# Products of two constant tiles ahead of waits in a two-layer hybrid decoder trunk

## The reference

```python
def _rmsnorm(x, w):
    return x * rsqrt(mean(x * x, axis=-1) + 1e-6) * w

def _layer(x, state, p):
    f = _swiglu(_rmsnorm(x, p['ffn1_norm_pre']), w_gate, w_up, w_down)     # 1024 -> 2816 -> 1024
    x = x + 0.5 * _rmsnorm(f, p['ffn1_norm_post'])
    m, new_state = _token_mixer(_rmsnorm(x, p['mix_norm_pre']), *state, p)
    x = x + _rmsnorm(m, p['mix_norm_post'])
    f = _swiglu(_rmsnorm(x, p['ffn2_norm_pre']), ...)
    x = x + 0.5 * _rmsnorm(f, p['ffn2_norm_post'])

def _token_mixer(h, ...):
    proj = h @ w_in
    # three recurrent branches over chunks of tokens, each with a state:
    # gated delta rule (4 heads), gated linear attention (4 heads), SSD (8 heads);
    # each output is normalised and gated
    merged = g0 * (o_gdn @ w_br_gdn) + g1 * (o_gla @ w_br_gla) + g2 * (o_ssd @ w_br_ssd)
    return merged @ w_out, new_state
```

## Time and profile before

| | |
|---|---|
| median of three runs | 3268.22 us |
| profiled execution | 3272.43 us |
| its span | 3270.6 us |
| mean granted clock of TensorE | 0.98 |
| PE busy | 3132.8 us, 96% |
| PEld busy | 3039.1 us, 93% |
| POOL busy | 1586.6 us, 49% |
| DVE busy | 1409.6 us, 43% |
| ACT busy | 769.3 us, 24% |

### The profile page before, as it was taken

The page is one execution under the profiler, slowest core; times in us unless marked ns, Lnnn a source line. Parts: engine busy times, 40 slices in busy tenths (PEclk is TensorE's granted clock), DMA queues, the critical chain, the costliest instruction groups (busy, mean ns, idle before and its releaser), DMA issues. The chain is left out here.

```text
span 3270.6 us, 66003 instructions
## 1 busy us (share of the span) xinstructions
PE 3132.8 (96%) x26830; PEld 3039.1 (93%) x26830; DVE 1409.6 (43%) x2212; ACT 769.3 (24%) x1515; POOL 1586.6 (49%) x948
## 2 busy tenths in 40 slices
PE   7999999999989999999999999999999899999998
PEld 7999999987779999999999999999877899999998
DVE  5332086647752225331153311955587522343312
ACT  2111033324441122111031110332344311221110
POOL 6655555600036554655555655655000356555553
PEclk9999999999979999999999999999999899999999
DMA  4222222200142221222222222222002323222222
GB/s 146 89 88 85 85 83 83 84 7 2 58 144 88 89 97 66 89 88 84 73 95 90 83 88 75 94 78 78 7 2 74 138 89 97 79 78 90 82 89 64
DMA packets 80595, 261.15 MB, mean 80 GB/s; under 512 B 8720, under 2 KB 12688, under 8 KB 79760
## 3 DMA queue, kind: packets, MB, share of 16 engines
q1 hardware_dynamic: 80112, 257.82, 23.9%
q10 hardware_dynamic: 288, 0.49, 0.1%
HBM read 243.70 MB, written 14.58 MB: 79 GB/s over the span
## 5 line engine op out<-in xcount | busy, mean ns | idle before, releaser
L620 POOL TENSOR_SCALAR wh<-raw 128x1024 fp32r<-128x1024 f32 (+2 forms) x236 | 243.5, 1032 | 1121.8 <-DMA raw<-in_merge 547.3
L622 POOL TENSOR_TENSOR wl<-raw,wh 128x1024 fp32r<-128x1024 f32 (+2 forms) x236 | 554.1, 2348 | 30.9 <-POOL wh L620 1.4
L622 POOL TENSOR_TENSOR wlx<-raw,whx 128x1024 fp32r<-128x1024 f32 (+2 forms) x236 | 546.7, 2316 | 30.9 <-POOL whx L620 0.2
L660 PE MATMUL ps<-hh,wh 128*128 128x272 f32 x2300 | 480.9, 290 | 27.8 <-POOL wl L622 12.8
L660 PE MATMUL ps<-hh,whx 128*128 128x272 f32 x2356 | 490.6, 290 | 0.0
L664 PE MATMUL ps<-hh,wlx 128*128 128x272 f32 x2356 | 487.2, 288 | 0.0
L662 PE MATMUL ps<-hl,whx 128*128 128x272 f32 x2356 | 487.0, 288 | 0.0
L664 PE MATMUL ps<-hh,wl 128*128 128x272 f32 x2300 | 477.3, 289 | 0.0
L662 PE MATMUL ps<-hl,wh 128*128 128x272 f32 x2300 | 477.0, 289 | 0.0
L620 POOL TENSOR_SCALAR whx<-raw 128x1024 fp32r<-128x1024 f32 (+2 forms) x236 | 243.5, 1032 | 469.6 <-PE ps L664 469.6
L660 PEld LDWEIGHTS ps<-hh,wh 128*128 128x128 f32 x2300 | 363.8, 190 | 30.5 <-issue 16.8
(11 more groups left out here) (450 smaller groups left out, 5276.5 us busy)
## 6 DMA issues: line engine op xcount, KB each, us to landing
raw<-in_up SPq DMA_DIRECT2D x176, 512.0 KB, 3.2
raw<-in_win SPq DMA_DIRECT2D x76, 512.0 KB, 3.2
raw<-in_merge SPq DMA_DIRECT2D x96, 384.0 KB, 3.0
raw<-in_down SPq DMA_DIRECT2D x64, 512.0 KB, 3.5
raw<-in_down SPq DMA_DIRECT2D x32, 384.0 KB, 3.1
raw<-in_wout SPq DMA_DIRECT2D x16, 512.0 KB, 3.2
states<-in_in_gdn SPq DMA_DIRECT2D x2, 2048.0 KB, 7.8
proj<-in_in_ssd SPq DMA_DIRECT2D x2, 2048.0 KB, 8.6
```

Source lines behind the costliest of these rows:

```text
L620: pool.tensor_scalar(hi, src, 1.0, 1.0, MULT, MULT).then_inc(hi_done, 1)
L622: pool.tensor_tensor(lo, src, hi.bitcast(F32), SUB).then_inc(lo_done, 1)
L660: pe.matmul(out, high, mh_[:, c], start=a, stop=False)
```

## The change

A helper `keep_busy(bank, count, c)` is added to PE's program. It multiplies `ones` (128x128) by the identity (128x128) in float32 `count` times, each into the same 128 columns of a bank of PSUM whose contents the next real product overwrites. It is called at these places: ahead of `first_tiles` (20 times, or 40 where the mixer ended), between the two calls of `add_squares` of half 1 (25 times, not where the mixer ended), ahead of `pre_stats` where the mixer ended (48 times), ahead of the recurrent part (40 times, with a wait for an earlier eviction first), and ahead of `sample_norm` (11 times). There the wait for `l_["s"]`, which used to be the second of two, now stands ahead of the 11 products, and the wait for the squares behind them. That makes 413 calls. Nothing else is changed.

```diff
+FILL_FFN, FILL_SQUARES, FILL_OUT, FILL_SUMS = 20, 25, 40, 48
+FILL_CHUNKS, FILL_NORM = 40, 11
...
+            def keep_busy(bank, count, c=0):
+
+                for _ in range(count):
+                    pe.matmul(ps[:, bank, c:c + P], ones, ident, start=True, stop=True, skip_group_check=True)
...
-            def post_stats(border, h):
+            def post_stats(border, h, filling=0):
                 pe.wait_ge(sums_added, post_added(border, ADDED_POST))
                 add_squares(h, sq[:, KD - 2, :], True, False)
+                keep_busy(1, filling)
                 pe.wait_ge(sq_ready, border * POST_SQUARES + KD + h)
                 add_squares(h, sq[:, KD - 1, :], False, True).then_inc(sum_ready, 1)
 
             def pre_stats(p):
+                if p % BORDERS == 2:
+                    keep_busy(0, FILL_SUMS, SPARE)
                 pe.wait_ge(sums_added, pre_added(p, ADDED_PRE))
...
             def first_tiles(layer, number, p, slots, first):
 
+                keep_busy(1, FILL_OUT if p % BORDERS == 2 else FILL_FFN)
                 for h in range(2):
...
-                            post_stats(p - 1, 1)
+                            post_stats(p - 1, 1, 0 if p % BORDERS == 2 else FILL_SQUARES)
...
             def sample_norm(step):
                 n, q = step.n, norm_number(step, 0)
                 yield
+                pe.wait_ge(l_["s"], step.once + 2)
+                keep_busy(4, FILL_NORM)
                 pe.wait_ge(n_["sq"], q)
-                pe.wait_ge(l_["s"], step.once + 2)
                 pe.matmul(ps[:, 4, 0:8 * n], ones, nsq_s[:, 0:8 * n], start=True, stop=True)
...
                 window(9, 3)
 
+                pe.wait_ge(evict_done, layer * 40 + 41)
+                keep_busy(0, FILL_CHUNKS)
                 pe.wait_ge(evict_done, value(pe, layer * 40 + 44))
```

## The result

The changed kernel took 3295.68 us, the median of four runs (3292.99 to 3297.73), beside 3267.27 for the kernel before (3265.36 to 3273.01): a ratio of 1.0077, 95% interval 1.0064 to 1.0090. Measured a second time, the ratio was 1.0092 (1.0079 to 1.0105). It is slower, as forecast, by 28.4 and 29.5 us where 20.1 had been summed. The profiled execution took 3297.73 with a span of 3295.9, 25.3 more than the span before.

The account below looks back on a forecast made before the run. PE, busy 96% of the span, was taken to bound the kernel; losses of 5.1 + 10.4 + 3.6 + 1.0 = 20.1 us on 3268.2 gave 3288 us, with bounds 3279 to 3302 and a given range of 3266 to 3304.

Parts of the forecast that it names:

- The price of a call: One added float32 product is two records, 0.223 us at full clock, making each fill some 1.7 times its wait.
- FFN borders: At p = 1, 3, 4 fills overrun their waits by more than the clock wins: 2.2, 0.7, 2.2 us lost, sum 5.1.
- Mixer borders: At p = 2 and 5 overrunning fills delay the first tiles and sum of squares: 5.2 us lost each, 10.4 in all.
- Starts of the recurrent part: Both layers: 40 calls make L1005 3.7 us late, full clock wins part back; 1.8 us lost each, sum 3.6.
- Norm of the sample tokens: Both layers: 11 calls take 4.7 us at half clock, mostly hidden by POOL holding DVE; 0.5 us each, sum 1.0.
- The total: Whole kernel: 5.1 + 10.4 + 3.6 + 1.0 = 20.1 us slower, forecast 3288 us.
- The step from the traced execution to the median: Profiled execution of before lies 4.2 us over the median, so 20.1 was added to 3268.2 rather than 3272.43.
- The range: All bounds' ends together: about +11 to +34 us, 3279 to 3302; the range given was 3266 to 3304.
- the first: Rival: at all filled waits a call takes 0.111 us and fills fit; 14.6 us faster, 3254 us; chance 12%.
- The second: Rival: waits behind L694 and L1060 absorb the delays, no change, about 3268 to 3274 us; chance 8%.
- third: Rival: constant products do not hold the clock at borders and recurrent starts, losses behind them stay; 3341 us; chance 4%.

Follow-up runs that it names:

- the half counts: Changed kernel with fills of 10, 12, 20, 24, 20 calls for 20, 25, 40, 48, 40, none ahead of the sample norm; 3259.04 us, again 3260.26.
- the transposes: Changed kernel with its 413 products made as transposes of the same two tiles, one record a call instead of two; 3261.20 us, ratio 0.9975.
- alone: Changed kernel with only the mixer borders' fills (40 and 48 calls), all other fills zero; 3283.59 us, ratio 1.0046.
- the experiment with 22 calls: Changed kernel with 22 instead of 11 calls ahead of the sample norm; 3293.84 us, one run.
- the fill that removes it: 9 calls ahead of the first sum of the keys' squares in each layer, added to halved fills without sample-norm calls; 3256.40 us, again 3254.31.
- the kernel without the FFN fills: Fills of 0, 0, 20, 24, 20 calls, none ahead of the sample norm, against the same kernel with 10 and 12 at FFN borders; 3261.12 us.

## Why the prediction was right, step by step

- *The price of a call* (0.223 us): the 80 and 96 records of a fill come 0.1116 us apart, 0.223 for a call. Right. That each fill overruns its wait follows, and the half counts and the transposes show that this alone sets the sign: -14.9 and -14.7 us at the borders and starts for fills that end in time, +18.5 for the full counts.
- *FFN borders*, 5.1 forecast, 5.03 measured. Right in each of the three, with the clock's gain and the overrun.
- *Mixer borders*, 10.4 forecast, 9.95 measured, and alone 9.94. The way it passed on is as argued: L690's four records, ACT's L1482, DVE's pace, then the sum and `sil`.
- *Starts of the recurrent part*, 3.6 forecast, 3.54 measured, both within the bounds of 0 and 3.7.
- *Norm of the sample tokens*, 1.0 forecast, 0.44 and 0.55 measured, for the reason given: the experiment with 22 calls shows the slack behind POOL used up. The fill took 4.32 us where 4.7 was counted at half clock throughout; in the trace the clock was back at 2.4 GHz from 950.4, within the fill, and low again from 957.3 to 964.1, at the merge's start.
- *The total*, 20.1 forecast, 25.3 in the traces and 28.4 and 29.5 in the medians. The steps were right and the list was short. The term that was left out is the clock at places that the change does not touch: 3.3 us behind the keys' sums, where the prediction had the clock "at half only at the recurrent parts' ends", shown by the fill that removes it and by the kernel without the FFN fills; and some 2 us net at the recurrent parts' ends (4.2 and -1.2 for the 1.0 forecast), where two traces of one kernel differ by more than that. The change's two traces agree here (both 4.2 and -1.2), but whether this part comes of the change was not tested. A further 0.8 us in the second FFN of layer 0 is there in nine of the twelve traces other than the first of before, and absent in three (one of the two of the half counts among them), with no tie to the fills that I can name.
- *The step from the traced execution to the median*: I took 4.2 us off the forecast because before's traced execution lay that far over its median, as if that were particular to this trace. The change's own traces lay 2.1 us over their median and right at it, and the second trace of before lay over its median again. That is the 3 to 4 us that the traces do not show; the clock of the 48 executions accounts for about 3 of them, the place stays open.
- *The range*: the lowest ends of the bounds add up to 13 us (5.1 + 8 + 0 + 0), not 11, so the lower end was 3281 and not 3279; the result lies far from it.
- *Rivals*: the first (a call of 0.111 us, 3254) is what the transposes and the half counts are, to 5 to 7 us; its mechanism was right for another form of call. The second and third did not come about.

## What to carry to other kernels

Work put into a wait to keep the clock has to end before the wait does: here 1.5 to 3 us were won at each border by fills that ended before the wait (0.35 and 0.58 us at the first), and 0.7 to 5 lost by the same fills at twice the length. It must not end too early either: with 1.5 to 3.7 us left idle the clock fell at most places. Take the price of the filler from rows of the same form and type (plain float32 costs two records a call, a transpose one), not from its number of columns. Put the filler ahead of the wait that ends last, and then look at the waits further on, since the clock may fall at one where it had not before.

## What the runs showed of the hardware

- Transposes of a 128x128 float32 tile, one record each 0.109 us, kept the granted clock at 2.4 GHz through waits of 2.6 to 6.4 us just as products did, and their time was the same within 2.2 us.
- A clock kept at one border led to a fall at a wait of 2.2 us some 0.1 ms later, twelve times of twelve, and a fall at the border spared it, ten times of ten. Each cost 1.6 us.
- Four DVE operations on 128x32 elements took 0.74 us with POOL idle and 4.52 beside two split blocks of POOL.
- Two executions of one kernel can differ by 5.9 us in one layer's recurrent part, with 13.7 us more of half clock in it.
- At the recurrent part's end, products of mostly 4 to 32 rows kept PE busy 82% of the time (20.5 us of layer 0 in the first trace of before; 81% in layer 1) at a granted clock of 0.50. Every trace has at least 17 us of low clock in a row there, in both layers, whatever was filled before. Whether the small products bring it about or the short waits among them (0.8 and 2.9 us) was not tested.
